# Norms turned with the identity instead of multiplied by a diagonal, and three steps placed elsewhere in the first block

## What is computed

```python
scores = jnp.einsum('bnqhd,bnkhd->bhnqk', qc, kc) * decay_mat[None, None]
intra = jnp.einsum('bhnqk,bnkhe->bnqhe', scores, vc)
```

```python
y = xf * lax.rsqrt(jnp.mean(xf * xf, axis=-1, keepdims=True) + EPS)
h = modulate(rms_norm_2(x, g_pre_mix[l]), sh1, sc1)     # y * g * (1 + scale) + shift
f = conv_ffn(modulate(rms_norm_2(x, g_pre_ffn[l]), sh2, sc2), w_up[l], ...)
```

## Time and profile before

| | |
|---|---|
| median of three runs | 1715.59 us (1715.35 to 1717.02) |
| the profiled execution's own time | 1715.31 us |
| span in the profile, first to last instruction | 1713.4 us |
| TensorE (PE) busy | 1672.2 us, 98% of the span |
| weight loads (PEld) busy | 1429.5 us, 83% |
| VectorE (DVE) busy | 1256.7 us, 73% |
| ScalarE (ACT) busy | 832.5 us, 49% |
| DMA | 148 GB/s read and written over the span |
| mean granted TensorE clock | 0.998 |

### The profile page before, as it was taken

How to read it: one execution, slowest core, us unless ns; L and a number is a source line. 1 busy time by engine, 2 the same in 40 slices (tenths; PEclk the granted TensorE clock), 3 DMA queues, 4 the chain that set the end, 5 groups by cost and what they waited for, 6 DMA issues and landing times.

```text
span 1713.4 us, 25211 instructions
## 1 busy us (share of the span) xinstructions
PE 1672.2 (98%) x9824; PEld 1429.5 (83%) x9824; DVE 1256.7 (73%) x2201; ACT 832.5 (49%) x1346; POOL 0.2 (0%) x4
## 2 busy tenths in 40 slices
PE   7999999999999999999999999999999999999998
PEld 7888888777787778889888888889778989979997
DVE  7899767774779798856877786347756786678774
ACT  6665545553324344344444442336453455466653
POOL 0000000000000000000000000000000000000000
PEclk9999999999999999999999999999999999999999
DMA  8646542231234344542545556224222344546553
GB/s 334 232 160 223 198 145 87 79 143 62 63 96 169 115 149 165 210 144 91 145 135 196 197 196 221 93 80 136 99 86 63 122 159 144 172 156 174 196 195 125
DMA packets 79078, 254.91 MB, mean 149 GB/s; under 512 B 14320, under 2 KB 18672, under 8 KB 78320
## 3 DMA queue, kind: packets, MB, share of 16 engines
q1 hardware_dynamic: 73488, 244.91, 42.7%
q10 hardware_dynamic: 5472, 8.39, 1.5%
HBM read 252.19 MB, written 1.07 MB: 148 GB/s over the span
## 4 chain that ended last, share of the span: by engine, by line
PE 79%; DVE 13%; ACT 4%; issue 3%; DMA 1%; ACTq 0%; DVEq 0%
PE bank L693 66%; DVE w_lo L1725 3%; PE bank L824 3%; PE bank L995 2%; PE bank L981 2%; PE bank L1073 2%; PE bank L972 2%; ACT w_hi L1180 1%; PE bank L786 1%; DVE mod_w L1780 1%; PE bank L1062 1%; DVE probT L1780 1%; DMA w_raw<-in_weights 1%; DVE att L2273 1%; DVE bank L2271 0%
## 5 line engine op out<-in xcount | busy, mean ns | idle before, releaser
L1725 DVE TENSOR_TENSOR w_lo<-w_raw,w_hi 128x1024 fp32r<-128x1024 f32 (+1 forms) x356 | 427.0, 1211 | 258.7 <-ACT w_hi L1180 257.1
L1180 ACT ACTIVATE w_hi<-w_raw 128x1024 fp32r<-128x1024 f32 (+1 forms) x356 | 370.0, 1048 | 343.8 <-PE bank L693 292.0
L693 PE MATMUL bank<-hT_hi,w_hi 128*128 128x512 f32 (+1 forms) x1280 | 446.0, 348 | 1.7 <-issue 0.6
L693 PE MATMUL bank<-hT_hi,w_lo 128*128 128x512 f32 (+1 forms) x1280 | 437.6, 342 | 0.0
L693 PE MATMUL bank<-hT_lo,w_hi 128*128 128x512 f32 (+1 forms) x1280 | 437.3, 342 | 0.0
L693 PEld LDWEIGHTS bank<-hT_hi,w_hi 128*128 128x128 f32 x1280 | 242.7, 190 | 30.2 <-issue 3.1
L693 PEld LDWEIGHTS bank<-hT_hi,w_lo 128*128 128x128 f32 x1280 | 242.6, 189 | 28.2
L693 PEld LDWEIGHTS bank<-hT_lo,w_hi 128*128 128x128 f32 x1280 | 242.8, 190 | 27.0 <-issue 1.0
L1780 DVE SCALAR_TENSOR_TENSOR mod_w<-mod_w,c_rows 128x1024 f32<-128x1024 f32 x96 | 117.0, 1219 | 7.0 <-DMA mod_w<-in_mod_weights 7.0
L693 PE MATMUL bank<-w_hi,hT_hi 128*128 128x512 f32 x272 | 114.6, 421 | 0.0
L693 PE MATMUL bank<-w_lo,hT_hi 128*128 128x512 f32 x272 | 106.6, 392 | 0.0
(11 more groups left out here) (370 smaller groups left out, 2787.5 us busy)
## 6 DMA issues: line engine op xcount, KB each, us to landing
w_raw<-in_weights SPq DMA_DIRECT2D x356, 512.0 KB, 4.0
mod_w<-in_mod_weights SPq DMA_DIRECT2D x96, 512.0 KB, 3.9
nbias<-in_window_bias ACTq DMA_DIRECT2D x32, 128.0 KB, 3.0
resid_c<-in_ctx ACTq DMA_DIRECT2D x2, 1024.0 KB, 5.4
gain_mix<-gain_rows SPq DMA_DIRECT2D x3, 512.0 KB, 5.9
gain_ffn<-gain_rows SPq DMA_DIRECT2D x3, 512.0 KB, 4.0
c_rows<-in_conditions SPq DMA_DIRECT2D x1, 1024.0 KB, 5.7
gatew<-in_gate_weights SPq DMA_DIRECT2D x1, 1024.0 KB, 11.5
```

Source lines behind the costliest of these rows:

```text
L693: mm = pe.matmul(held[key][:, oc], st, mv_, start=(opens and k == 0 and t == 0 and i == 0), stop=(closes and k == tiles - 1 and t == 2), s ...
L1180: a.activation(w_hi[:, p % RING, :, used], w_raw[:, p % RING, :].rearrange("p (k n) -> p k n", k=KP)[:, :, used], ACT.Copy).then_inc(hi_re ...
L1725: v.tensor_tensor(w_lo[:, p % RING, :, used], w_raw[:, p % RING, :].rearrange("p (k n) -> p k n", k=KP)[:, :, used], w_hi[:, p % RING, :, ...
```

## The change

Norms of the second block: the row scaling is done on the rows themselves. ScalarE writes columns 0 to 511 of a tile (`norm_left`), VectorE columns 512 to 1023 (`norm_right`, in place of the diagonal), into a buffer `rows_of` (`sg` in the first mixer norm, `normed_rows` in the second, `o_mix` for the FFN norms). TensorE transposes those blocks with the identity, waits for the left halves before pair 0 and for the right halves before pair 2.

```diff
             def norm_T(l, which, gi, pool="rot"):
                 of = groups(l, which)[gi]
-                for t in of:
-                    pe.wait_ge(*diag_ready.at((l, which, t)))
                 for p in range(KD // 2):
+                    if p % 2 == 0:
+                        for t in of:
+                            pe.wait_ge(*(right_ready if p else left_ready).at((l, which, t)))
...
-                            mm = pe.matmul(ps[:, o:o + P], resid[t // 2][:, t % 2, k * P:(k + 1) * P], diag[:, t, :],
-                                           start=True, stop=True)
+                            mm = pe.transpose(ps[:, o:o + P], rows_of(l, which, t)[:, k * P:(k + 1) * P], ident)
...
+            def norm_left(l, which, t):
+                act.wait_ge(*A.last())
+                act.wait_ge(*inv_ready.at((l, which, t)))
+                a.activation(rows_of(l, which, t)[:, 0:COLS], resid[t // 2][:, t % 2, 0:COLS], ACT.Copy, scale=ss[:, 4 + t:5 + t])\
+                    .then_inc(*A.tell(left_ready, (l, which, t)))
...
+            for t in range(NT):
+                norm_left(0, "mix", t)
             split_hi(LAST_OUT + 2)
...
                 norm_root(0, "mix", 2 + t, sg[:, t, :])
                 split_hi(LAST_OUT + 6)
+                norm_left(0, "mix", 2 + t)
...
                                 norm_root(*nxt, t, o)
+                                if not final:
+                                    norm_left(*nxt, t)
                             if final:
                                 split_hi(after + 4)
-                                for gi, p in ((0, 2), (0, 3), (1, 0), (1, 1), (1, 2), (1, 3)):
+                                norm_hi(*nxt, 0, 2)
+                                norm_left(*nxt, t)
+                                for gi, p in ((0, 3), (1, 0), (1, 1), (1, 2), (1, 3)):
                                     norm_hi(*nxt, gi, p)
...
-            def norm_diag(l, which, t):
+            def norm_right(l, which, t):
                 dve.wait_ge(*root_ready.at((l, which, t)))
-                v.reciprocal(ss[:, 4 + t:5 + t], rs[:, 56 + t:57 + t]).then_inc(*W.next())
+                v.reciprocal(ss[:, 4 + t:5 + t], rs[:, 56 + t:57 + t]).then_inc(*W.tell(inv_ready, (l, which, t)))
                 dve.wait_ge(*W.last())
-                v.tensor_scalar(diag[:, t, :], ident, ss[:, 4 + t:5 + t], None, ALU.mult)\
-                    .then_inc(*W.tell(diag_ready, (l, which, t)))
+                v.tensor_scalar(rows_of(l, which, t)[:, COLS:D], resid[t // 2][:, t % 2, COLS:D], ss[:, 4 + t:5 + t], None, ALU.mult)\
+                    .then_inc(*W.tell(right_ready, (l, which, t)))
```

```diff
             for g in range(KD // 2):
-                split_lo(g)
+                split_lo(g + 1)
                 dve.wait_ge(*xT_hi_ready.at(g))
...
             for i in range(2, 4):
                 conv_pair(i)
-                split_lo(9 + i)
+                split_lo(10 + i)
...
             split_lo(24)
+            dve.wait_ge(decay_loaded, 16)
+            ret_decay(0)
             mod_ops(2)
             split_lo(25)
             mod_ops(2)
             split_lo(26)
-            dve.wait_ge(decay_loaded, 16)
-            ret_decay(0)
```

More of the change, by code:

```diff
@@ L193, in build @@
     o_mix = sb("o_mix", [P, 2 * NT, D], S)
+    normed_rows = sb("normed_rows", [P, 2 * NT, D], S + 8 * KB)
     merged = sb("merged", [P, KD, TT], S)
@@ L256, in build @@
     nqT_lo = [sb(f"nqT_lo{j}", [P, TT], rows_at + (4 + 2 * j) * KB if j < 3 else R + 38 * KB, F32R) for j in range(4)]
-    diag = sb("diag", [P, 2 * NT, P], rows_at + 8 * KB)
     conv = sb("conv", [P, 4, TT], rows_at)
@@ L300, in normed_pair, with rows_of @@
         return x[:, of[0] // 2, 2 * p:2 * p + 2, of[0] % 2 * P:of[0] % 2 * P + len(of) * P]
+    def rows_of(l, which, t):
+        if which == "mix":
+            return normed_rows[:, t, :] if l else sg[:, t % 2, :]
+        return o_mix[:, t, :]
     def ntmp_pair(l, which, gi, p):
@@ L487, in build @@
     xn_ready = Counter("xn_ready")
-    diag_ready = Counter("diag_ready")
+    inv_ready = Counter("inv_ready")
+    left_ready = Counter("left_ready")
+    right_ready = Counter("right_ready")
     yT_hi_ready = Counter("yT_hi_ready")
@@ L500, in build @@
                qk_root, qk_ss, resid_ready, ret_hi, ret_root, ret_var, ret_y, root_ready, rows_ready, xT_hi_ready,
-               xT_ready, xn_ready, diag_ready, yT_hi_ready, yT_ready, gcol_ready, stat_ready, zo_ready, eps_ready)
+               xT_ready, xn_ready, inv_ready, left_ready, right_ready, yT_hi_ready, yT_ready, gcol_ready, stat_ready, zo_ready, eps_ready)
     by_name = {c.name: c.sem for c in signals}
@@ L2080, in _ @@
             for t in range(NT):
-                norm_diag(0, "mix", t)
+                norm_right(0, "mix", t)
             split_lo(LAST_OUT)
@@ L2107, in _ @@
                 split_lo(LAST_OUT + 5)
-                norm_diag(0, "mix", 2 + t)
+                norm_right(0, "mix", 2 + t)
             norm_second(0, "mix")
@@ L2157, in post @@
                             split_lo((piece("w_up", l, 0) if which == "mix" else piece("w_in_2", l + 1, 0)) + 1)
-                        norm_diag(*nxt, t)
+                        norm_right(*nxt, t)
                     if final:
```

## The result

| | before | changed |
|---|---|---|
| median (us) | 1715.49 of 6 runs (1715.35 to 1717.76) | 1723.55 of 6 runs (1721.68 to 1725.14) |
| profiled execution, its span | 1715.31, 1713.4 | 1724.05, 1722.3 |
| TensorE busy, records | 1672.2, 9824 | 1667.0, 9712 |
| mean granted TensorE clock | 0.998 | 0.992 |

Ratio 1.0043, 95% interval 1.003 to 1.0056: slower by 8.1 us between the medians. The prediction said 1716.0 with a range of 1709.5 to 1721. TensorE was relieved by 112 records as foreseen, and yet the end came 8.9 us later in the profiles.

A forecast was written before the change was run, and what follows sets the result against it. TensorE was taken as the bound (79% of the ending chain), VectorE from 80 to 181 us. Norms +0.15, low halves -1.8, decay product +2.1: +0.45 on 1715.31 us, plus 0.3 to the median: 1716.0; range 1709.5 to 1721.

The forecast's parts named there:

- the walk through the FFN norm of layer 0: Around 784 to 798 us: tile 2's copy delays the weight piece 0.86 us, second half starts turning later; net -0.75 us.
- The mixer norm of layer 1: First half's VectorE chain moves 0.3 us, second half starts 1.2 later, then saves 1.8; net -0.1 us.
- The FFN norm of layer 1: One-tile groups save only 0.9 us a half; the chain TensorE already awaited moves 0.86; net +0.8 us.
- The first mixer norm: From 209 us: saved turning becomes a longer wait for a low half, VectorE's pairs set the pace; net +0.2 us.
- The duration: ScalarE's new 128x512 scaled copy in each norm was taken to occupy 0.55 to 0.9 us of its queue.
- The turning: Norms: transposing 112 blocks instead of multiplying takes 12.8 us off TensorE, a ceiling reached only if it never waits there.
- Rival (a): Clock falls after waits in the norms: up to 2.9 us each; one (1718.9 us) chance 0.22, two or more 0.16.
- (b): Transposes don't keep the clock up, so it falls in all four norms: 1727.6 us; chance 0.04.
- (c): First block: the decay product gives back what TensorE's stall cost, a gain up to 6.5 us: 1707.4; chance 0.1.
- (d): Norms' saved TensorE time carries through: about half of 12.8 us gives 1709.6, all with the low halves 1703; chance 0.1.
- the decay product: First block, near 91 us: made earlier, TensorE's stall goes but VectorE waits 1.65 us for a high half; +2.1 us.
- the low halves: First block: two low halves of weight pieces made earlier on VectorE, removing TensorE's wait at 46 us; together -1.8 us.

The follow-up runs named there:

- experiment 6: Changed kernel, but VectorE scales whole rows (128x1024) and ScalarE makes no copy: 1717.42 us, ratio 1.0008 against the kernel before.
- experiment 12: Kernel before plus ScalarE's fourteen scaled half-row copies, read by nobody; TensorE still multiplies by the diagonal: 1722.16 us, ratio 1.0038.
- experiment 10: Kernel before with two low halves moved; in each norm diagonal for the first tile group, whole rows on VectorE and transposes for the second: 1713.97 us, ratio 0.9991.
- filled waits: Changed kernel with dummy identity products in TensorE's four long waits, 12 in three norms and 8 in the first mixer norm: 1720.67 us, ratio 1.0025.
- the norms alone: Changed kernel with the first block's three edits taken back: 1721.64 us, ratio 1.0033 against the kernel before.
- the low halves alone: Kernel before with only the two low halves of weight pieces moved in the first block; decay product and norms as before: 1713.82 us, ratio 0.999.

## Why the prediction was wrong

- **The step that failed** is the walk through the FFN norm of layer 0: "the new copy of tile 2 (783.70 to 784.33) stands before the weight piece in ScalarE's queue, so the piece starts at 784.24, 0.86 us later". It looked at the last copy alone. Three tiles pass through ScalarE ahead of that point, each with a copy, and each step of ScalarE that finds its input ready waits behind a copy that itself waits for VectorE's inverse. The copies of tiles 0 and 1 cost 1.3 us together, tile 2's 1.0 (shown by the rows, and as a sum by experiments 6 and 12). 0.86 was 2.3, TensorE's wait 4.33 instead of 3.0, and the norm, put at -0.75, cost 2.82.
- **The same mistake in the other norms.** The mixer norm of layer 1 was put at -0.1 and is +1.63; there the prediction moved the chain by 0.3 us. The FFN norm of layer 1, +0.8, was nearly right at +0.99: only one tile passes ahead of its start, so there the walk over one copy was the whole walk. The first mixer norm, put at +0.2 and measured at +0.93, is another matter: the longer wait at 221 us was foreseen, the fall of the clock behind it was not, and by my estimate it is 0.6 of the 0.93.
- **The duration** was nearly right: 0.72 us for the copy and 0.29 of wait ahead of it, 1.0 of ScalarE's queue in all, just above the 0.55 to 0.9 assumed. It was the number of copies in the chain that was wrong.
- **The turning** saved TensorE's time as computed, but its share that gets through is smaller than the 1.8 us counted for a second half: 0.6 in the FFN norm of layer 0 (experiments 6 and 10), and 0.2 at most in layer 1 (experiment 6, mixer norm). The fourth bank is the limit, which the prediction did not look at.
- **Rival (a)** named the second mechanism, and its condition (waits beyond those of the earlier trace rows) came true in all four norms: 4.33 and 3.47 us where 3.0 and 2.4 were walked, but also 2.31 and 2.95 where 2.9 and 3.1 were. Its price was wrong: up to 2.9 us a fall was put; filled waits show 1.2 us for the one at 790 and nothing for the three others. The 2.9 took the work as halved in speed; the counts beside it, 7 products in a microsecond against 10, give 1.7. With the estimated 0.6 for the fall from 224 the clock explains a fifth of the loss, not the loss.
- **Rivals (b), (c), (d)** did not happen: transposes kept the clock; the decay product gave nothing for its stall; little of the turning carried through.
- **The first block was right** in each step: -1.54 (for -1.8) from the low halves, +1.76 (for +2.1) from the decay product, together +0.47 in the profile at 211 us (for +0.3), with both waits where they were forecast.
- **The sum by its terms**: norms 6.4 instead of 0.15, first block 0.5 instead of 0.3, and 1.9 us that I had no term for. Of these, 1.26 arise near 1055, all but 0.2 as a wait of TensorE for the high half that follows. The piece that SyncE asks for at 1050.38 is awaited by ScalarE until 1058.38; before, 6.8 us lay between the same two steps, now 8.0.

```profile
1050.38 0.43 SPq L643 DMA_DIRECT2D w_raw<-in_weights  x1
...
1058.38 1.06 ACT L1189 ACTIVATE w_hi<-w_raw 128x1024 fp32r<-128x1024 f32 x1 [8.75 <-DMA w_raw<-in_weights]
```

It was late in the norms alone too (+1.08) and not with unused copies or filled waits (-0.02, +0.15), so it does not follow from the new copies as such. With rows on VectorE the load took 8.15 us too, and TensorE did not wait for it (+0.14). The 0.68 us arise near 1370, where ScalarE issues six loads of `nbias` before a weight piece. The first two issues, in the changed kernel and then before:

```profile
1371.63 1.50 ACTq L1527 DMA_DIRECT2D nbias<-in_window_bias  x2
```

```profile
1364.54 0.82 ACTq L1504 DMA_DIRECT2D nbias<-in_window_bias  x2
```

The piece behind the six starts after 2.63 us instead of 1.94. Why the load and the issues take longer in some kernels stays open.

## What to carry to other kernels

An operation put into an in-order queue costs there at every pass, with its wait for the producer included: walk the whole loop that leads to the critical point, not its last turn. Two checks are cheap: add the new operations with nobody reading them, and move them to the engine that idles at that moment. And where a faster step refills buffers, look at who empties them before counting the saving.

Of the kernels run here the one to keep is the low halves alone: 0.999 (0.9981 to 0.9999) of before, 1713.8 us.

## What the runs showed of the hardware

- The 128x512 scaled copy between fp32 tiles takes ScalarE 0.72 us; VectorE scales 128x512 in 0.49 us and 128x1024 in 0.75 us, so half a row each was no gain over a whole row on VectorE. In the changed kernel, ScalarE's copies in the FFN norms (duration in ns, least, median, most):

```profile
L1353 ACT ACTIVATE o_mix<-resid_x,ss x4: 721/722/727, 786.4 to 1529.7; 128x512 f32<-128x512 f32 x4
```

- A wait of TensorE of about 2.2 us is followed by a fall of the clock in one kernel and by none in another with the same rows around it. The wait of 1.80 us at 221 is followed by a fall in the changed kernel and by none in the norms alone. A wait of 4.33 us in front of the first product of the layer 0 FFN norm gave a fall of 6.8 us in the changed kernel and of 3.4 in the norms alone. One execution of each kernel can't price such a wait.
- A fall costs only where TensorE sets the pace behind it: 1.2 to 1.5 us near 240 in kernels that multiply by the diagonal, 1.2 at 790, nothing at 241, 1162 and 1524 in the changed kernel.
